# x token-major by block transposes on VectorE and a round trip through DRAM, in place of transposes on TensorE

## The reference

```
zxbcdt = h @ w_in                                  # z 2048, x 2048, B 512, C 512, dt 32 columns
xbc = silu(causal_dwconv(xbc, conv_w, conv_b))     # 4 taps along the tokens
# 4 groups of 8 heads of 64 channels, state 128, 4 chunks of 128 tokens
xdt = x * dtc[..., None]
cb = einsum("bclgn,bcsgn->bcgls", cc, bc)
y_diag = einsum("bcgls,bcgrls,bcsgrp->bclgrp", cb, decay, xdt)
states = einsum("bclgn,bcgrl,bclgrp->bcgrpn", bc, decay_to_end, xdt)
# scan over the chunks: h = h * chunk_decay + states
y = y_diag + y_off + d_skip * x
y = grouped_rms_norm(y * silu(z)) * norm_g @ w_out
```

## Time and profile before

| | us |
|---|---|
| median of 3 runs | 1106.39 (1106.36 to 1106.46) |
| the profiled execution | 1106.54 |
| its span | 1104.7 |
| PE busy | 1092.8 |

### The profile page before, as it was taken

How to read it: one execution, slowest core, us unless ns; L and a number is a source line. 1 busy time by engine, 2 the same in 40 slices (tenths; PEclk the granted TensorE clock), 3 DMA queues, 4 the chain that set the end, 5 groups by cost and what they waited for, 6 DMA issues and landing times.

```text
span 1104.7 us, 15384 instructions
## 1 busy us (share of the span) xinstructions
PE 1092.8 (99%) x5168; PEld 899.8 (81%) x5168; DVE 577.3 (52%) x644; ACT 474.2 (43%) x816; POOL 610.8 (55%) x460
## 2 busy tenths in 40 slices
PE   9999999999999999999999999999999999999997
PEld 7788888888888788888887888888888888888886
DVE  5665421455432384676777866666664124554123
ACT  7433222233333338458595785343332222333332
POOL 3866544444566635537466376656665444445653
PEclk9999999999999999999999999999999999999999
DMA  7223232222222225333334233222222222333232
GB/s 286 79 99 105 86 103 97 96 95 95 96 95 95 96 77 152 123 112 124 117 104 143 105 125 106 96 95 96 95 95 96 95 95 95 97 99 101 93 104 77
DMA packets 40085, 117.05 MB, mean 106 GB/s; under 512 B 4080, under 2 KB 11888, under 8 KB 40048
## 3 DMA queue, kind: packets, MB, share of 16 engines
q1 hardware_dynamic: 39616, 115.83, 31.3%
q10 hardware_dynamic: 432, 0.73, 0.2%
HBM read 114.32 MB, written 2.23 MB: 105 GB/s over the span
## 4 chain that ended last, share of the span: by engine, by line
PE 93%; ACT 2%; DVE 1%; POOL 1%; issue 1%; DMA 1%; ACTq 0%; DVEq 0%; POOLq 0%
PE bank L857 30%; PE bank L859 29%; PE bank L858 29%; PE bank L1048 1%; PE bank L1057 1%; DMA params<-params 1%; ACT m L634 1%; PE bank L898 1%; PE bank L1007 0%; ACT w_hi L445 0%; POOL w_lo L729 0%; POOL residual L756 0%; PE bank L878 0%; PE bank L1025 0%; ACT y_accumulated L609 0%
## 5 line engine op out<-in xcount | busy, mean ns | idle before, releaser
L729 POOL TENSOR_TENSOR w_lo<-w_raw,w_hi 128x512 fp32r<-128x512 f32 x372 | 497.5, 1343 | 442.5 <-ACT w_hi L445 429.9
L445 ACT ACTIVATE w_hi<-w_raw 128x512 fp32r<-128x512 f32 x372 | 230.5, 626 | 383.0 <-PE bank L859 373.5
L857 PE MATMUL bank<-x_hi,w_hi 128*128 128x512 f32 x848 | 331.9, 391 | 1.8 <-DVE x_lo L1159 1.5
L859 PE MATMUL bank<-x_hi,w_lo 128*128 128x512 f32 x848 | 330.2, 389 | 0.0
L858 PE MATMUL bank<-x_lo,w_hi 128*128 128x512 f32 x848 | 330.1, 389 | 0.0
L857 PE MATMUL bank<-act_hi,w_hi 128*128 128x512 f32 (+1 forms) x656 | 252.9, 386 | 0.0
L859 PE MATMUL bank<-act_hi,w_lo 128*128 128x512 f32 (+1 forms) x656 | 251.8, 384 | 0.0
L858 PE MATMUL bank<-act_lo,w_hi 128*128 128x512 f32 (+1 forms) x656 | 251.8, 384 | 0.0
L857 PEld LDWEIGHTS bank<-x_hi,w_hi 128*128 128x128 f32 x848 | 159.2, 188 | 37.5 <-issue 2.8
L859 PEld LDWEIGHTS bank<-x_hi,w_lo 128*128 128x128 f32 x848 | 159.2, 188 | 33.1
L858 PEld LDWEIGHTS bank<-x_lo,w_hi 128*128 128x128 f32 x848 | 159.3, 188 | 32.6
(11 more groups left out here) (161 smaller groups left out, 725.8 us busy)
## 6 DMA issues: line engine op xcount, KB each, us to landing
w_raw<-weights SPq DMA_DIRECT2D x186, 512.0 KB, 3.3
m<-acs_scratch SPq DMA_DIRECT2D x16, 512.0 KB, 4.4
decay_in<-eacs_scratch SPq DMA_DIRECT2D x24, 128.0 KB, 3.8
x_token<-x_tok SPq DMA_DIRECT2D x4, 512.0 KB, 6.4
residual<-xt SPq DMA_DIRECT2D x8, 256.0 KB, 10.1
out_first<-scaled_residual SPq DMA_DIRECT2D x4, 256.0 KB, 2.4
out_second<-output_rows SPq DMA_DIRECT2D x4, 256.0 KB, 2.7
pooling_matrices<-pooling ACTq DMA_DIRECT2D x2, 288.0 KB, 5.2
```

Source lines behind the costliest of these rows:

```text
L445: act.activation(whi[:, c % 2, part], raw[:, c % 2, part], ACT.Copy).then_inc(hi_ready, 1)
L729: pool.tensor_tensor(wlo[:, c % 2, part], raw[:, c % 2, part], whi_f[:, c % 2, part], ALU.subtract).then_inc(lo_ready, 1)
L857: pe.matmul(out, wh, xh, start=start, stop=False)
L859: return pe.matmul(out, wl, xh, start=False, stop=stop)
```

## The change

x comes to token-major form on another way. DVE transposes 32 x 32 blocks of the activated x into `y_accumulated` (`transpose_blocks`), four DMAs write them to a DRAM scratch (`write_blocks`), one reads them back with tokens on the partitions (`read_tokens`), and `token_x` on DVE reads that instead of PSUM, in two instructions per chunk. PE's transposes of x go. For this the four x tiles of a group are computed ahead of B and C, and the silu of x moves to slot 8 of the previous group. `skip`, which overwrites the place where x landed, moves from slot 0 to slot 3. ACT makes the first exponent ahead of the squares; DVE makes the first `x_dt` and the first `m` ahead of the others; POOL makes the first decayed x behind the sums of squares, and a half unit of weights ahead of its rest. The state products were in rounded parts before and stay so.

The diff, with what the change speaks of; line numbers, semaphore names and unchanged lines are left out:

```diff
@@
...
         acs_dram = nc.dram_tensor("acs_scratch", [GROUPS, CHUNKS, HPG, P], F32).ap()
+        x_dram = nc.dram_tensor("x_scratch", [GROUPS, CHUNKS * (P // Q), Q, P // Q, GT * Q], F32).ap()
         eacs_dram = nc.dram_tensor("eacs_scratch", [GROUPS, CHUNKS, HPG, P], F32).ap()
...
         b_misc, b_yd, b_yo, b_st, b_stat = bank[3], bank[4], bank[5], bank[6], bank[7]
-        XT_BANK = (b_yd, b_yo, b_st, b_misc)
 
@@
...
 
+        def x_blocks(g):
+
+            return yx[:, GT * g:GT * g + GT, :].rearrange("p i t -> p (i t)").rearrange("p (n f) -> p n f", f=GT * Q)
+
         def conv_out(n):
...
             g, q = divmod(n, CONVS)
-            return bf[:, :] if q == 0 else cf[:, g % 2, :] if q == 1 else xact[:, q - 2, :]
+            return xact[:, q, :] if q < GT else bf[:, :] if q == GT else cf[:, g % 2, :]
 
@@
...
                                  heads[:, half, :, :].to_broadcast([64, GT, P])).then_inc(e_landed[c % 2], 16)
+
+            def write_blocks(g):
+
+                sp.wait_ge(xt_blocks, g + 1)
+                blocks = x_blocks(g)
+                for a in range(P // Q):
+                    sp.dma_start(x_dram[g, :, :, a, :].rearrange("n q f -> q n f"),
+                                 blocks[Q * a:Q * a + Q, :, :]).then_inc(xt_written, 16)
+
+            def read_tokens(g):
+
+                sp.wait_ge(xt_written, 16 * (P // Q) * (g + 1))
+                sp.dma_start(yx[:, GT * g:GT * g + GT, :],
+                             x_dram[g].rearrange("(c b) q a f -> (b q) c (a f)", c=CHUNKS)
+                             ).then_inc(xt_landed, 16)
 
@@
...
                 load_ahead(u)
+            write_blocks(0)
             sp.wait_ge(acsf_ready, 1)
@@
...
             load_ahead(5)
+            read_tokens(0)
             sp.wait_ge(scratch, 2 * GROUPS * 16)
@@
...
                         load_exp_acs(g, 1)
+                    if t == 8 and g + 1 < GROUPS:
+                        write_blocks(g + 1)
+                    if t == 9 and g + 1 < GROUPS:
+                        read_tokens(g + 1)
             with sp.Fori(0, (UNITS - U_MLP1 - 2) // 2) as i:
@@
...
 
+            def silu_x(g):
+                act.wait_ge(acc_drained, A_SSM + conv_slot(CONVS * g + GT - 1) + 1)
+                act.activation(xact[:, :, :], xact[:, :, :], ACT.Silu).then_inc(x_act, 1)
+
             for u in range(CONVS):
@@
...
                     act.activation(eacs_f[:, :], acs_f[:, :], ACT.Exp).then_inc(decays, 1)
+                if u == 4:
+                    silu_x(0)
                 first_tap(u)
@@
...
 
-                for q in range(2):
+                for q in range(GT, CONVS):
                     act.wait_ge(acc_drained, A_SSM + conv_slot(CONVS * g + q) + 1)
...
 
-            def silu_x(g):
-                act.wait_ge(acc_drained, A_SSM + conv_slot(CONVS * g + CONVS - 1) + 1)
-                act.activation(xact[:, :, :], xact[:, :, :], ACT.Silu).then_inc(x_act, 1)
-
             def skip(g):
 
-                act.wait_ge(x_act, g + 1)
+                act.wait_ge(xdt_ready, 4 * g + 4)
                 for i in range(GT):
@@
...
                     u = slot_of(g, t)
+                    if not ends and t == 8:
+                        silu_x(g + 1)
+                    ahead(u, 0)
                     if t == 2:
                         decayed_hi(g, 0)
-                    ahead(u, 0)
                     if t == 0:
                         silu_b_c(g)
-                        silu_x(g)
                         if g:
@@
...
                         first_tap(CONVS * (g + 1) + t - GT)
-                    if t == 0:
+                    if t == 3:
                         skip(g)
+                    if t == 1:
+                        exp_segments(g, FALL_IN[t])
                     if t == 1 and g:
...
                         root(SSM_STAT + g - 1, group_root)
-                    if t in FALL_IN:
+                    if t in FALL_IN and t > 1:
                         exp_segments(g, FALL_IN[t])
@@
...
                     u = slot_of(g, t)
-                    if t == 2:
-                        decayed(g, 0)
                     if t == 2 and g:
...
                     if t == 2:
+                        decayed(g, 0)
+                    split_half(U_SSM + u + 2, 0)
+                    if t == 2:
                         decayed_lo(g, 0)
-                    split_half(U_SSM + u + 2, 0)
                     if t in (4, 6):
@@
...
 
-            def token_x(g, c):
-
-                for i in range(GT):
-                    last = pe.transpose(XT_BANK[c][:, P * i:P * i + P], xact[:, i, P * c:P * c + P], ident)
-                last.then_inc(x_mm, 1)
-
             def token_major(g):
...
                 if g:
-                    pe.wait_ge(xdt_ready, 4 * g)
+                    pe.wait_ge(bt_lo_ready, g)
                 for c in range(CHUNKS):
@@
...
                 last.then_inc(cb_mm, 1)
-                pe.wait_ge(x_act, g + 1)
-                if g == 0:
+
+            def c_chunk(g, c):
+                return cf[:, g % 2, P * c:P * c + P]
+
+            def chunk(g, c):
+
+                pe.wait_ge(m_ready, 4 * g + c + 1)
+                pe.wait_ge(xdt_ready, 4 * g + c + 1)
+                if g == 0 and c == 0:
                     pe.wait_ge(acsf_ready, 1)
                 else:
-                    pe.wait_ge(y_add, 4 * g)
-                    pe.wait_ge(y_dec, 3 * g)
-                    pe.wait_ge(state_ready, 3 * g)
-                for c in range(CHUNKS - 1):
-                    token_x(g, c)
-
-            def c_chunk(g, c):
-                return cf[:, g % 2, P * c:P * c + P]
-
-            def chunk(g, c):
-
-                pe.wait_ge(m_ready, 4 * g + c + 1)
-                pe.wait_ge(xdt_ready, 4 * g + c + 1)
-                if c:
                     pe.wait_ge(y_add, 4 * g + c)
@@
...
                     pe.wait_ge(state_ready, 3 * g + c)
-                    if c > 1:
+                    if g or c > 1:
                         pe.wait_ge(y_dec, 3 * g + c - 1)
@@
...
                     pe.wait_ge(bt_lo_ready, g + 1)
-                    if c == 0:
-                        pe.wait_ge(xdt_ready, 4 * g + 3)
+                    if g and c == 0:
+                        pe.wait_ge(state_ready, 3 * g)
                     three(b_st[:, :], bt_hi[:, c, :], bt_lo[:, c, :], dec_hi[:, :], dec_lo[:, :], True, True
@@
...
                         token_major(g)
-                    if t == T_LATE_TOKEN:
-                        pe.wait_ge(bt_lo_ready, g + 1)
-                        token_x(g, CHUNKS - 1)
                     if t == T_STAT and g:
@@
...
                                              ).then_inc(acc_drained if k == 0 else conv_step, 1)
+
+            def transpose_blocks(g):
+
+                dve.wait_ge(x_act, g + 1)
+                blocks = x_blocks(g)
+                for i in range(GT):
+                    last = dve.transpose(blocks[:, :, Q * i:Q * i + Q],
+                                         xact[:, i, :].rearrange("p (n j) -> p n j", j=Q))
+                last.then_inc(xt_blocks, 1)
 
@@
...
                 conv_scale(u)
+                if u == 4:
+                    transpose_blocks(0)
                 conv_taps(u)
@@
...
 
-                dve.wait_ge(x_mm, 4 * g + c + 1)
-                dve.tensor_tensor(by_head(xdt[:, c, :]), by_head(XT_BANK[c][:, :]),
-                                  of_group(dt_t[:, :, :].rearrange("p c h -> p (c h)"), c, g, HD), ALU.mult
-                                  ).then_inc(xdt_ready, 1)
+                dve.wait_ge(xt_landed, 16 * (g + 1))
+                if g and c == 0:
+                    dve.wait_ge(yd_ready, 4 * g)
+                    dve.wait_ge(dec_ready, 3 * g)
+                out = xdt[:, c, :].rearrange("p (i h a j) -> p h i a j", h=2, a=2, j=Q)
+                landed = yx[:, GT * g + c, :].rearrange("p (h a i j) -> p h i a j", h=2, a=2, j=Q)
+                dt = dt_t[:, c, HPG * g:HPG * g + HPG].rearrange("p (i h) -> p h i", h=2)
+                for half in range(2):
+                    last = dve.tensor_tensor(out[:, half], landed[:, half],
+                                             dt[:, half].unsqueeze(2).unsqueeze(3).to_broadcast([P, GT, 2, Q]),
+                                             ALU.mult)
+                last.then_inc(xdt_ready, 1)
 
@@
...
                         token_x(g, 0)
-                        token_x(g, 1)
-                        token_x(g, 2)
-                        b_token_lo(g)
-                    if t == 3:
-                        token_x(g, 3)
+                        decay_times_cb(g, 0)
                     if t == T_STAT + 1 and g:
@@
...
                         conv_scale(CONVS * (g + 1) + t - GT)
+                        if t == 8:
+                            transpose_blocks(g + 1)
                         if t == T_STAT and g:
...
                     if t == 2:
-                        decay_times_cb(g, 0)
```

(8 more changed lines are left out.)

11 lines of the change are left out of this document (7 added, 4 removed).

## The result

| | before | after |
|---|---|---|
| median of 4 runs each, us | 1106.38 | 1118.84 (1117.25 to 1120.32) |
| the profiled execution, its span | 1106.54, 1104.7 | 1120.16, 1118.3 |

The ratio is 1.0112, with a 95% interval from 1.0094 to 1.0131. The forecast was 1111.2 with a range up to 1116.0, so the direction was right and the size was not: the span grew by 13.6 us where 4.8 were summed. The four executions of the changed kernel fall into two pairs, 1117.25 and 1117.52 us at a mean granted clock of 0.994, and 1120.16 and 1120.32 at 0.992, and the profile is of one of the second pair.

A forecast was written before the change was run, and what follows sets the result against it. PE was taken as full (busy 1092.8 of 1104.7 us), with an equally long chain over POOL, ACT and DVE behind it. Groups 0 to 3 gave +0.5, +1.8, +1.5, +1.0, together +4.8: 1106.5 to 1111.2, range 1101.5 to 1116.

The forecast's parts named there:

- The removed transposes: On PE, 16 transposes fewer per group save 1.7 us with a start-up cost, 6.7 us in all.
- The waits for decayed_lo: PE's state product, chunk 0: waits of 2.0 and 2.7 us in groups 1 and 2, 2.7 in 3, 1.2 in 0.
- The term for the port: x_dt with two SBUF inputs contends with POOL, adding 1.1 us (bounds 0 and 1.5) to each chunk-0 wait.
- The waits for `m` at chunk 2: PE waits 1.5 us in groups 1 and 2, in group 2 in place of 1.0 before; none in group 3.
- `m` at E+43.7: Group 2, chunk 2: `m` ready 43.7 us after PE begins to transpose B; PE arrives at 42.2 and waits 1.5.
- Group 2: -1.7 - 1.0 + 2.7 + 1.5 = +1.5: Group 2: transposes removed, old `m` wait gone, new chunk-0 wait, new chunk-2 wait; net 1.5 us slower.
- Silu of c in group 0: Last input of PE's step in group 0, ready at 429.1 instead of needed at 428.11: PE waits 1.0 us.
- Block transposes and DRAM: Four DVE transposes take 2.4 us per group; DRAM write and read of x cost nothing in groups 1 to 3.
- Rival C: Slower still: x lands late from DRAM, 1150 us, or block transposes take 5 us, 1116; chance 0.1.
- the bound of 5 us for the transposes: Upper bound for DVE's four block transposes of the next group, twice 2.4 to 3.0 for four-byte data.
- rival A: Waits small: no DVE-POOL blocking, 0.9 us at each chunk 0, chunk-2 chain about 1 later; 1106.1, no change; chance 0.25.
- B: Faster: DVE and POOL finish in time at chunk 0, most of 6.7 us kept; 1099.8 to 1104; chance 0.2.

The follow-up runs named there:

- e6_route_alone: Changed kernel with the old orders on ACT and POOL, so only the new way of x: 1121.2 us, 1.0132 of the kernel before.
- e11_later_dt_mlast: Changed kernel with PE's state product of chunk 0 later, dt read from PSUM, and the product with `m` last in a chunk: 1116.41 us.
- e12_later_mlast: Changed kernel with PE's state product of chunk 0 later and the product with `m` last in a chunk: 1117.13 us.
- e7_m_first: Changed kernel with group 0's load of `m` put ahead of a load of weights and the read of x on SP: 1120.18 us.
- e16_m2_alone: Changed kernel with `m` of chunk 2 made one slot ahead on DVE: 1113.7 us.
- e2_dt_psum: Changed kernel with x_dt of chunks 1 to 3 reading the step sizes from PSUM, and B's unused chunk-3 transposes left out: 1117.39 us.
- e1_fill: Changed kernel with 12, 6, 12 and 17 useless matmuls on PE ahead of its wait for decayed_lo in the four groups: 1116.1 us.
- e4_both: Changed kernel with dt read from PSUM and POOL's three sums of squares moved behind slot 2's work: 1114.8 us.

## Why the prediction was right or wrong, point by point

- **The removed transposes**: kept. The account with 6.7 closes within 1.3 us in the nine kernels for which it is given here, which is also how far it can be trusted; `e6_route_alone` is 1.7 off by the same sum, and `e11_later_dt_mlast` and `e12_later_mlast` nearly 4.
- **The waits for decayed_lo**: the mechanism was right in all four groups, the total 10.9 against 8.6. Group 1 was 1.5 (2.0 forecast), group 2 2.5 (2.7), group 3 4.0 (2.7), group 0 2.8 (1.2). Group 0 was mis-sized because the load of `m` (4.0 us of waiting on ACT) and then a load of weights (1.1), which the prediction names as queued behind SP's waits and prices at nothing, both landed late; the late read of x (3.0 on DVE) was covered. Group 3 is longer than group 2 for two reasons that the timelines show. PE is there 13.6 us after its transposes of B (640.92) and not 14.1 (568.76), since it has not waited 0.55 for `m`. And decayed_lo ends 17.6 us after them and not 16.5: ACT, having waited 0.67 for weights, begins the exponent 0.8 later, and POOL's work from the sums on takes 0.3 longer. Which of these went in `e7_m_first` and `e16_m2_alone`, where group 3 waited 2.45 and 2.44, no run isolates.
- **The term for the port**: right in kind (x_dt halves of up to 1.52 us against 1.5 forecast), too large in effect: 0.5 us on POOL's chain, not 1.1 (`e2_dt_psum`).
- **The waits for `m` at chunk 2**: group 1 had 1.51 against 1.5. Group 2 had 0.15, mainly because the lower clock held PE back; when `e1_fill` took that away, it was 1.54. So both terms were right in what the chain could bear. (The prediction gives no terms for its "`m` at E+43.7" of group 2; it came at E+44.2, 613.00 - 568.76.)
- **The step that failed** is the sum's silent assumption that a wait costs its own length. "Group 2: -1.7 - 1.0 + 2.7 + 1.5 = +1.5", and the like for the others, have no term for TensorE's clock. It measured 5.9 us, two thirds of the 8.8 by which the span missed. What the runs put in its place: a wait of 2.27 us or more costs 1.7 to 3.0 us more behind it in 27 of 28 cases, and the wait's length does not say which. One of 4.09 (`e7_m_first`) cost 1.7, one of 2.42 (`e2_dt_psum`, clock 0.50 over 6 us) 3.0. So the term could be forecast in kind, but not to the us.
- **A wait that I had not seen**: y_accumulated at chunk 3, 2.1 us in two groups. I took PE's arrival there as harmless without reading DVE's slack in the trace of before (y_accumulated ends at 549.63, PE is there at 550.20), which one stretched instruction used up.
- **Silu of c in group 0**, costed at 1.0: no such wait. The transposes began at 415.8, not at 417.0, since the silu of x came earlier than I placed it.
- **Block transposes and DRAM**: 0.67 us each against 0.6, and x was late in group 0 alone. Rival C's mechanisms did not occur, nor did the bound of 5 us for the transposes; rival A and B fell with the waits at chunk 0.
- **Cause**: 2.3 (decayed_lo) + 2.1 (y_accumulated) + 5.9 (clock) - 1.0 (silu) - 0.6 (`m`) = 8.7 of the missing 8.8. The direction was no luck, since the waits that the forecast named came; without the clock the span would have missed by about 2.9 us. (The 1111.2 of the forecast adds its 4.8 to the median; from the profiled 1106.5 it is 1111.3.) What stays open is why no arrangement got the 6.7 us: the runs show a next wait each time, on four chains, but no kernel without any.

## What to carry to other kernels

When the bounding engine is full and chains behind it have 0.5 us of slack (here `m` at chunk 2 and y_accumulated at chunk 3), work taken off it buys waits, and a wait on TensorE must be priced with the matmuls that run at half rate behind it. Before shortening a chain that is waited for, see whether the waiting instruction can stand half a unit later: that one edit gave 6.4 us, those on the chain 4.0 at best (`e4_both`). After each repair read the list of waits again, since the gain is what the next one lets through.
